# A stick-breaking attention trunk: the weights of six heads turned by VectorE and DRAM transfers instead of TensorE

## What is computed

```python
log_beta = jax.nn.log_sigmoid(z)                      # z = scaled q.k
log_skip_j = jnp.where(causal, jax.nn.log_sigmoid(-z), 0.0)
log_skip = lax.cumsum(log_skip_j, axis=3, reverse=True) - log_skip_j
weights = jnp.where(causal, jnp.exp(log_beta + log_skip), 0.0)
outs.append(jnp.einsum('bhts,bhsd->bhtd', weights.astype(vb.dtype), vb))
```

## Time and profile before

| | |
|---|---|
| timed runs | 1175.13, 1175.51, 1175.27 us, median 1175.27 us |
| profiled execution, span from first to last instruction | 1173.5 us |
| median over that span | 1.8 us |
| PE, DVE, ACT, POOL busy | 1163.8, 796.7, 419.7, 149.8 us |
| attention steps 0 to 5 | from about 84 to 463 us of the span |

### The profile page before, as it was taken

One profiled execution on the slowest core, in us unless ns is written; L12 is line 12 of the kernel. 1 busy time (PEld: TensorE's weight loads), 2 busy tenths in 40 slices (PEclk: granted clock), 3 DMA queues, 4 the chain that ended last, 5 costly groups with the idle time before them and its releaser, 6 DMA issues. The chain is left out here.

```text
span 1173.5 us, 20148 instructions
## 1 busy us (share of the span) xinstructions
PE 1163.8 (99%) x7228; PEld 1071.4 (91%) x7228; DVE 796.7 (68%) x1612; ACT 419.7 (36%) x911; POOL 149.8 (13%) x344
## 2 busy tenths in 40 slices
PE   8999999999999999999999999999999999999998
PEld 8999999999999999888888989898999999999787
DVE  5757485766767675774444778788888888788421
ACT  5535353545445454452222222323232322222200
POOL 2422121203031211110003100000000000000000
PEclk9999999999999999999999999999999999999999
DMA  8210223223142301066632110314142421117441
GB/s 251 57 53 19 73 82 112 68 83 103 67 119 73 109 1 46 1 228 218 209 108 73 55 36 20 115 66 137 70 145 72 133 86 45 45 37 296 148 139 72
DMA packets 110659, 113.51 MB, mean 97 GB/s; under 512 B 6880, under 2 KB 86752, under 8 KB 110560
## 3 DMA queue, kind: packets, MB, share of 16 engines
q1 hardware_dynamic: 110560, 112.23, 30.1%
HBM read 79.70 MB, written 32.51 MB: 96 GB/s over the span
## 5 line engine op out<-in xcount | busy, mean ns | idle before, releaser
L28 PE MATMUL p_proj<-w_qkv_hi,ut_hi 128*128 128x384 f32 x504 | 172.0, 341 | 0.2 <-DVE ut_lo L796 0.2
L30 PE MATMUL p_proj<-w_qkv_hi,ut_lo 128*128 128x384 f32 x504 | 169.1, 336 | 0.0
L29 PE MATMUL p_proj<-w_qkv_lo,ut_hi 128*128 128x384 f32 x504 | 168.7, 335 | 0.0
L28 PE MATMUL p_proj<-w_ig_hi,next_hi 128*128 128x256 f32 x512 | 145.5, 284 | 0.0
L29 PE MATMUL p_proj<-w_ig_lo,next_hi 128*128 128x256 f32 x512 | 143.1, 279 | 0.0
L30 PE MATMUL p_proj<-w_ig_hi,next_lo 128*128 128x256 f32 x512 | 143.0, 279 | 0.0
L28 PE MATMUL p_proj<-next_hi,w_qf_hi 128*128 128x512 f32 x282 | 113.2, 402 | 0.0
L30 PE MATMUL p_proj<-next_hi,w_qf_lo 128*128 128x512 f32 x282 | 110.1, 390 | 0.0
L29 PE MATMUL p_proj<-next_lo,w_qf_hi 128*128 128x512 f32 x282 | 109.8, 390 | 0.0
L808 DVE TENSOR_TENSOR_SCAN a_skip<-a_skip,a_diagonal 128x129 f32<-128x129 f32 (+3 forms) x64 | 86.9, 1358 | 30.2 <-ACT a_beta L648 28.4
L28 PEld LDWEIGHTS p_proj<-w_ig_hi,next_hi 128*128 128x128 f32 x512 | 96.2, 188 | 0.0
(11 more groups left out here) (255 smaller groups left out, 2732.3 us busy)
## 6 DMA issues: line engine op xcount, KB each, us to landing
stage<-in_hg_w_in_dram SPq DMA_DIRECT2D x32, 512.0 KB, 4.3
stage<-in_sb_w_in_dram SPq DMA_DIRECT2D x29, 512.0 KB, 5.9
w_out_hi_scratch<-m_in SPq DMA_DIRECT2D x32, 256.0 KB, 2.1
w_out_lo_scratch<-m_in SPq DMA_DIRECT2D x32, 256.0 KB, 2.3
m_in<-mixed_scratch SPq DMA_DIRECT2D x12, 448.0 KB, 6.1
a_beta<-in_x_dram SPq DMA_DIRECT2D x8, 512.0 KB, 4.3
m_in<-in_sb_w_out_dram SPq DMA_DIRECT2D x16, 256.0 KB, 3.6
ut_hi<-w_out_hi_scratch SPq DMA_DIRECT2D x8, 512.0 KB, 8.7
```

Of the source, the lines that this page charges most:

```text
L28: pe.matmul(out, w_hi, m_hi, start=start, stop=False, skip_group_check=True)
L29: pe.matmul(out, w_hi, m_lo, start=False, stop=False, skip_group_check=True)
L30: return pe.matmul(out, w_lo, m_hi, start=False, stop=stop, skip_group_check=True)
```

## The change

For heads 0 to 5 (`CARRIED` = 6) the turn on PE goes. Instead, in use i, right behind the weights of tile i, DVE transposes `beta` in 32 by 32 blocks into `skip` (`flip`); SP stores that tile to a DRAM scratch (`flips`), waits until it has landed, waits for `o_done` of the pair before, and loads it back with four transfers into `wt_lo`, so that the blocks come to lie on the right partitions (`carry`). Ahead of the scores of use i + 2, ACT rounds from `wt_lo` into `wt_hi` (`settle_weights`) and DVE subtracts in place (`refine_weights`). The value products keep their places behind uses 3, 5, 7 and 9, now with moving operands in runs of 32 columns. The loads of projection weights for heads 2 to 7 go from SP's program to ACT's. The splitting of output weights moves from uses 5, 6, 7, 9 to uses 1, 2, 3, 4, and its transfers stand between the carries in SP's program. Heads 6 and 7 keep the turn on PE, with the new layout of `wt_hi` and `wt_lo`. The semaphores `row_loaded` are shared by both layers.

```diff
+    flips = nc.dram_tensor("flips_scratch", (TILES, P, SEQ), F32).ap()
...
-    PLAIN = {"before": {i: [("scores", 0, i)] for i in range(TILES)},
-             "after": {i: ([("outputs", 0, (i - 3) // 2)] if i >= 3 and i % 2 == 1 else []) +
-                       ([("turn", 0, i - 1)] if 1 <= i <= TILES else []) for i in range(USES)}}
+    PLAIN = {"before": {i: ([("settle", 0, i - 2)] if i >= 2 else []) +
+                        ([("scores", 0, i)] if i < TILES else []) for i in range(USES)},
+             "after": {i: [("outputs", 0, (i - 3) // 2)] for i in range(3, USES, 2)}}
...
-    SPLIT_AT = [5, 6, 7, 9]
+    SPLIT_AT = [1, 2, 3, 4]
+    QUARTER = P // 4
+    CARRIED = HEADS - 2
...
-        wt_hi = sb("wt_hi", [P, TILES, 2, P], F32R)
-        wt_lo = sb("wt_lo", [P, TILES, 2, P], F32R)
+        wt_hi = sb("wt_hi", [P, 2, 4, TILES, QUARTER], F32R)
+        wt_lo = sb("wt_lo", [P, 2, 4, TILES, QUARTER], F32R)
...
+            def carry(h, j):
+                sp.wait_ge(flipped, TILES * h + j + 1)
+                run = (j + 1) * QUARTER
+                sp.dma_start(flips[j, :, 0:4 * run], skip[j % 2][:, 0:4 * run]).then_inc(flip_stored[j % 2], 16)
+                sp.wait_ge(flip_stored[j % 2], 16 * (PAIRS * h + j // 2 + 1))
+                if j >= 2 or not known_first(h):
+                    sp.wait_ge(o_done, PAIRS * h + j // 2)
+                for c in range(4):
+                    dst = wt_lo[c * QUARTER:(c + 1) * QUARTER, j % 2, :, 0:j + 1, :].bitcast(F32)
+                    sp.dma_start(dst.rearrange("p g s i -> p g (s i)"),
+                                 flips[j, :, c * run:(c + 1) * run].rearrange("(g p) r -> p g r", g=4)
+                                 ).then_inc(carried[j % 2], 16)
+            def carry_and_split(h, group):
+                load_raw_half(sp, m_in, w_out, link, group, 0)
+                load_raw_half(sp, m_in, w_out, link, group, 1)
+                carry(h, 0)
+                carry(h, 1)
+                store_half(sp, m_in, w_out, link, group, 0)
+                load_raw_half(sp, m_in, w_out, link, group, 2)
+                store_half(sp, m_in, w_out, link, group, 1)
+                load_raw_half(sp, m_in, w_out, link, group, 3)
+                carry(h, 2)
+                store_half(sp, m_in, w_out, link, group, 2)
+                carry(h, 3)
+                store_half(sp, m_in, w_out, link, group, 3)
+                for j in range(4, TILES):
+                    carry(h, j)
+                for i in range(2):
+                    sp.wait_ge(link["w_parts_stored"][i], group * 64 + 64)
...
-            for p in range(4):
-                load(2, p)
+            for j in range(TILES):
+                carry(0, j)
             store(0, 0)
-            for p in range(4):
-                load(3, p)
             with sp.Fori(0, 2) as pair:
                 for b in (1, 0):
-                    split_and_store(sp, m_in, w_out, link, pair * 2 + 1 - b)
+                    carry_and_split(pair * 2 + 2 - b, pair * 2 + 1 - b)
                     store(pair * 2 + 2 - b, b)
-                    for p in range(4):
-                        load(pair * 2 + 5 - b, p)
+            for j in range(TILES):
+                carry(HEADS - 3, j)
             store(HEADS - 3, 1)
...
-                        if i >= 2:
-                            act.wait_ge(weights_turned, UNITS * h + ENDS[i - 2])
-                        elif not known_first(h):
-                            act.wait_ge(weights_turned, UNITS * (h - 1) + ENDS[i + 6])
+                        if is_carried(h) or h == CARRIED and i < 2:
+                            if i >= 2 or not known_first(h):
+                                act.wait_ge(flip_stored[i % 2], 16 * (PAIRS * h + i // 2))
+                        elif i >= 2:
+                            act.wait_ge(weights_turned, turned_units(h, ENDS[i - 2]))
+                        else:
+                            act.wait_ge(weights_turned, turned_units(h - 1, ENDS[i + 6]))
...
+                    elif what == "settle":
+                        for u in range(Z_UNITS[tile]):
+                            settle_weights(head, tile, u)
...
+            def settle_weights(h, j, u):
+                act.wait_ge(carried[j % 2], 64 * (PAIRS * h + j // 2 + 1))
+                blocks = unit_blocks(j, u)
+                act.activation(wt_hi[:, j % 2, :, blocks, :], wt_lo[:, j % 2, :, blocks, :].bitcast(F32),
+                               ACT.Copy).then_inc(wt_hi_ready, 1)
...
+                    if plan is FIRST and i == USES - 1:
+                        for p in range(3):
+                            load(2, p)
...
+                    if plan is PLAIN and i == 5:
+                        load(h + 2, 3)
+                    if plan is PLAIN and i == USES - 1 and not (isinstance(h, int) and h == HEADS - 3):
+                        for p in range(3):
+                            load(h + 3, p)
...
+            def flip(h, i):
+                width = (i + 1) * P
+                dve.wait_ge(weights_ready, TILES * h + i + 1)
+                dve.transpose(skip[i % 2][:, 0:width].rearrange("p (c s i) -> p s c i", c=4, i=QUARTER),
+                              beta[i % 2][:, 0:width].rearrange("p (s c i) -> p s c i", c=4, i=QUARTER)
+                              ).then_inc(flipped, 1)
...
+            def refine_weights(h, j, u):
+                dve.wait_ge(wt_hi_ready, UNITS * h + ENDS[j] - Z_UNITS[j] + u + 1)
+                part = (slice(None), j % 2, slice(None), unit_blocks(j, u), slice(None))
+                dve.tensor_tensor(wt_lo[part], wt_lo[part].bitcast(F32), wt_hi[part].bitcast(F32),
+                                  ALU.subtract).then_inc(wt_ready, 1)
...
+                o_quarters = p_o[:, :, :].rearrange("p a (g i) -> p a g i", i=QUARTER)
                 for s in range(2 * g + 2):
-                    o = p_o[:, :, :] if s <= 2 * g else p_o[:, 1, :]
-                    w_h = wt_hi[:, s, :, :] if s <= 2 * g else wt_hi[:, s, 1, :]
-                    w_l = wt_lo[:, s, :, :] if s <= 2 * g else wt_lo[:, s, 1, :]
+                    tiles = slice(0, 2) if s <= 2 * g else 1
+                    o = o_quarters[:, tiles, :, :]
+                    w_h = wt_hi[:, tiles, :, s, :]
+                    w_l = wt_lo[:, tiles, :, s, :]
```

51 lines of the change are left out of this document (34 added, 17 removed).

## The result

The changed kernel takes 1206.76 us (median of four runs, 1204.93 to 1208.60), the kernel before 1175.39 us: ratio 1.0266, 95% interval 1.0252 to 1.0281. The forecast was 1184.9 us: the sign was right, the size a third of what came. The later runs of the kernel before, beside each group of experiments, have medians of 1175.2 to 1175.5 us.

The account below looks back on a forecast made before the run. PE, busy 99% of the span, was taken as the bound. Waits of 34.8 us less 25.2 gone gave +9.6 on the 1173.5 us span, 1183.1; with 1.8 for timed runs, 1184.9 us, range 1171 to 1205.

Parts of the forecast that it names:

- The waits: PE's new waits in heads 0 to 5: 7.2 us in four split heads, 3.0 in two plain ones, 34.8 us.
- the split head's first wait: Second unit of tile 5's scores: tile 2's store, behind the fourth half's load, makes PE wait 1.8 us.
- The forecast's 1.3 us at pair 1: Split head, pair 1's products: tile 3's store stands behind two more stores, DVE's refinement behind a half's subtraction; 1.3 us.
- The clock: PE's clock expected to stay full, with waits of 2 us among 60, with no row for it.
- What goes: PE's 36 transposes a head at 0.098 us plus 0.08 for each of 8 tiles: 4.2 us, 25.2 in six heads.
- Rival 4: Value products: PE reads weights slower in runs of 32 columns, 4 to 21 us on top, 1189 to 1206; chance 0.04.
- the waits of a plain head: PE waits 2.0 us at pair 2, 0.5 at pair 1, 0.5 at pair 3, none at pair 0: 3.0 us.
- pair 2's wait on DVE's order: Pair 2's products wait 2.0 us, as tile 5's subtraction stands behind DVE's scan, product, flip, squares and values.
- The flip: DVE's transpose of 128 to 1024 columns per tile: 1.1 us for tile 6, 5.8 us a head.
- The carry: Store, landing and four loads of a tile: about 4.1 us from first issue to whole tile, at any size.
- ACT's weight loads: Weight loads moved to ACT cost nothing, issued a head ahead; without that cover 9 us would come in.
- Case 3: Dearer steps: flip at the scan's pace, 1201, or landings 0.6 us later on every carry, 1199; chance 0.18.

Follow-up runs that it names:

- the reordered kernel: Changed kernel with SP carrying tiles 0 to 3 before the halves' stores, and halves 2 and 3 split at the ends of uses 7 and 8; 1182.13 us.
- without halves: Changed kernel with the splitting of the first layer's output weights left out in the steps of heads 1 to 4; 1176.28 us.
- with the sigmoids alone moved: Changed kernel with its own SP order, ACT making the new even tile's sigmoids before copying the carried tile; 1192.35 us.
- the kernel with the values on ACT and POOL: From the reordered kernel, ACT rounds the values and POOL takes their remainders, instead of DVE; 1186.64 us.
- the gate's load one use earlier: Reordered kernel with sigmoids of even tiles first, and ACT's 512 KB gate load at the end of use 4, not 5; 1183.22 us.
- the filler: Changed kernel with the first product of tile 5's first scores made 19 times instead of once in heads 1 to 4; 1213.14 us.
- three edits of DVE's and ACT's work, in five kernels: On the reordered kernel: tile 5's split earlier, ACT issuing two loads, both; values on ACT and POOL, alone and with both: 1181.63, 1181.67, 1181.84, 1186.64, 1183.49 us.
- the last kernel: Reordered kernel with sigmoids of even tiles first, and SP's loads of halves 2 and 3 issued behind tile 5's carry; 1172.68 us.
- the kernel with two flips: From the reordered kernel, DVE makes each flip twice, one behind the other; 1194.39 us.

## Why the prediction failed

Forecast +9.6 us in the profiled span, measured +29.7 (1203.2 - 1173.5). By the two pages the 29.7 are 38.1 more of PE standing still and 8.4 less of PE busy; the busy part is 9.4 for the clock, by the reordered kernel, and -17.8 for the work. Against the forecast's terms:

- **The waits, 34.8 us forecast, 38.1 measured.** The total was near, its parts were not. The step that failed is the split head's first wait, "the load of the fourth half, then the store of tile 2. That is issued about when pair 0's products end (T)": it went out at T + 3.2, and the wait was 3.5 to 5.8 us instead of 1.8. I had priced the halves' landing at 2.3 once, from a quiet stretch. SP meets it twice between tile 1's loads and tile 2's store, at the third half's load (2.5) and at the fourth's (3.6), one behind the other. The kernels without halves and with the other order show that it is this stretch. The forecast's 1.3 us at pair 1 did not come, being in the first wait already: where that wait is short, with the sigmoids alone moved, pair 1 has its 2.2 to 3.9.
- **The clock, 0 forecast, 9.4 measured.** "Waits of 2 us among 60 I expect to leave it there": that was on the edge of what the runs bear out (last section), and four of the five drops followed the mis-sized wait of 3.5 to 5.8 us. The two steps are for the most part one error that was paid twice.
- **What goes, 25.2 us forecast, 17.8 measured.** Taken as distances between starts, less the waits, in a head of the reordered kernel against one before, the 36 transposes gave 3.3 us, 0.09 each, where the forecast had 3.5. The step behind them, 0.64 us a head in the forecast, did not go: scores are 0.1 us shorter and the projection's products 0.2 longer. And the value products take 0.29 us longer (from first to last start 2.07 for 1.94 at pair 2, 2.79 for 2.65 at pair 3, 0.01 more each at pairs 0 and 1). That makes 3.0 us a head.
- **Rival 4, slower reading in runs of 32 columns: hardly there.** Of the 0.29 us, 0.21 is the first distance at pairs 2 and 3. It is 0.22 to 0.23 us where PE stood just before, and 0.12 where it did not, as before the change. The rest, products 0.120 us apart instead of 0.118, is 0.08 us a head, 0.5 in six, where the rival's smaller price was 4. Pair 2 of the changed kernel, head 1, and of the kernel with the values on ACT and POOL, head 4:

```profile
182.53 0.39 PE L28 MATMUL a_p_o<-a_wt_hi,a_v_hi 128*128 128x256 f32 x1 [1.52 <-DVE a_wt_lo L935]
182.76 0.28 PE L29 MATMUL a_p_o<-a_wt_lo,a_v_hi 128*128 128x256 f32 x1
```

```profile
375.01 0.28 PE L28 MATMUL a_p_o<-a_wt_hi,a_v_hi 128*128 128x256 f32 x1
375.12 0.28 PE L29 MATMUL a_p_o<-a_wt_lo,a_v_hi 128*128 128x256 f32 x1
```

- **Right:** the waits of a plain head (3.1 us in head 5 for 3.0), though it takes 63.6 us and not 63, as less work went; pair 2's wait on DVE's order in every head, at 1.5 us for 2.0, and that its price is the flip's; ACT's longest waits are for the carries.
- **The flip: right.** Its row for all 48: `311/778/1246` ns for the shortest, the median and the longest (128 and 1024 columns), 1.1 us for tile 6. Between the ends that is 1.04 ns a column. The microarchitecture page of the Trainium skill (Vector Engine (DVE) Microarchitecture Reference, 3.8) has one element per cycle per lane; by that rule the slope agrees, and the fixed 0.18 us comes on top.
- **The carry: 4.1 us on the whole, but not "at any size".** From first issue to whole tile is 1.3 us to the last issue and one landing: 3.1 to 3.2 us for tile 1 (median landing 1.8) and 4.4 to 4.6 for tile 7 (3.0). The first is under the 3.5 us that the prediction named as a sign of being wrong; the waits do not hang on it. Short runs cost nothing to see: the median landing is 1.7 us for loads of 16 KB in runs of 128 B and 2.1 for 64 KB. The Trainium skill (DMA: Bandwidth & Descriptors, Specifications) has a read-modify-write there; these landings do not show one.
- **ACT's weight loads "cost nothing on this path": wrong as a rule.** Moved to use 6 the same loads cost 21 us. Where they stood they delay tile 0's store, and PE's waits do not follow that delay (head 3).

Of the rivals none took place as written. Case 3 was nearest, dearer steps by landings behind other traffic, but its 0.6 us on every carry was 1.7 to 4.0 us more of one wait in each split head, and that came with the clock.

Two things stay open. Why the gate's load one use earlier costs 4.7 us was not followed up; pair 2's waits of 2.7 to 3.4 us in three heads say where. And whether the clock would stay full with the waits of the changed kernel otherwise in place was tried once (the filler) and not answered.

## What to carry to other kernels

A work item moved to DMA can have the order of a queue's program as its main price, here 24.6 of 31.4 us: list what its queue waits for between its transfers, with landing times taken next to the traffic that will be there, before adding up engine time. Put latency-bound round trips ahead of bulk transfers that only a later stage wants, and let an engine do what frees another before it stands at what arrives late. And a microsecond taken from one wait should be followed to the next: here three edits of DVE's and ACT's work, in five kernels, took from the wait at pair 2 or 3 and gave it back within the head.

## What the runs showed of the hardware

- Counted over the attention steps of all the kernels here: behind every wait of PE of 3.13 us or more (33 of them) the granted clock went to 1.2 GHz for 3.4 to 10.2 us, from 2 to 5 us after the wait's start; behind none of 1.76 us or less; between these sometimes (after 1.77 in the last kernel, not after 3.09 in the one with the gate's load a use earlier). Such a stretch costs half of PE's busy time in it: 9.4 us of 18.8 in the changed kernel, where 8.5 of the 27.3 us lay inside the waits; and PE is busy 8.9 us longer in the kernel with two flips, of whose 17.1 us at this clock it fills 16.5.
- Tile 1's store of 128 KB has a median landing of 1.9 us, tile 0's of 64 KB one of 3.9, up to 5.9 behind 2.5 MB that were issued in the 6 us before it, and 2.0 in head 3, where the last of them were issued 5 us before. The DMA share over these steps was 0.45 where it had been 0.24.
- The first of a run of value products (256 columns) stands 0.22 to 0.23 us ahead of the second when PE stood before it, and 0.12 when it did not.
- DVE's 32 by 32 transposes of float32 take 0.31 us for 128 columns and 1.25 for 1024.
